# Packing the heads' sums and root broadcasts into quarters of TensorE, and swapping the rotation's halves by DMA, in a two-layer hybrid decoder

## The reference, cut to what matters

```python
def _head_rmsnorm(y, g, n_heads):
    yh = y.reshape(b, l, n_heads, w // n_heads)
    yh = yh * lax.rsqrt(jnp.mean(yh * yh, axis=-1, keepdims=True) + NORM_EPS)
    return yh.reshape(b, l, w) * g
# mLSTM, for each head:
    num = s @ v                                   # s: masked scores x weights
    den = sum(s, axis=-1)
    h_cell = num / maximum(abs(den), exp(-m_t))
# retention turns its queries and keys, halves (x1, x2) of each head:
    x1 * cos - x2 * sin,  x1 * sin + x2 * cos
# gated outputs, and the merge of the four branches:
    silu(r) * norm(gla);  sigmoid(o) * norm(h_cell);  silu(g) * norm(ret)
    merged = sum_n sigmoid(logits[n] + b) * (branch[n] @ w_branch[n])
```

## Time and profile before

| | |
|---|---|
| median of 3 runs | 1001.17 us (1001.13 to 1002.32) |
| the profiled execution, its own time | 1002.59 us |
| its span, first to last instruction | 1000.8 us |
| TensorE, matmuls | 984.6 us busy, 98% of the span |
| TensorE, weight loads | 933.9 us |
| VectorE | 592.3 us, 59% |
| ScalarE | 519.9 us, 52% |
| GpSimd | 85.0 us, 8% |
| DMA | 156.43 MB, 156 GB/s on the mean |
| granted clock of TensorE, mean | 0.996 |

### The profile page before, as it was taken

How to read it: one execution, slowest core, us unless ns; L and a number is a source line. 1 busy time by engine, 2 the same in 40 slices (tenths; PEclk the granted TensorE clock), 3 DMA queues, 4 the chain that set the end, 5 groups by cost and what they waited for, 6 DMA issues and landing times.

```text
span 1000.8 us, 19677 instructions
## 1 busy us (share of the span) xinstructions
PE 984.6 (98%) x7722; PEld 933.9 (93%) x7722; DVE 592.3 (59%) x903; ACT 519.9 (52%) x832; POOL 85.0 (8%) x78
## 2 busy tenths in 40 slices
PE   8999999999999999999999999999999999999997
PEld 6999888889998999999979998888999899999996
DVE  7556565356866655553465565744578566556443
ACT  5543754365466544444455437544754755555442
POOL 1000000000031221110100000000000322221010
PEclk9999999999999999999999999999999999999999
DMA  6864434346552655555545544344464546565551
GB/s 179 280 209 142 125 114 126 91 121 168 170 172 84 207 168 170 173 191 163 165 127 168 169 145 126 110 126 127 128 168 169 169 128 209 171 202 172 190 189 42
DMA packets 168525, 156.43 MB, mean 156 GB/s; under 512 B 9092, under 2 KB 167023, under 8 KB 168079
## 3 DMA queue, kind: packets, MB, share of 16 engines
q1 hardware_dynamic: 167598, 152.13, 49.2%
q10 hardware_dynamic: 672, 3.37, 1.0%
q0 software_dynamic: 192, 0.07, 0.0%
HBM read 154.50 MB, written 1.05 MB: 155 GB/s over the span
## 4 chain that ended last, share of the span: by engine, by line
PE 92%; DVE 3%; ACT 3%; DMA 1%; issue 1%; DVEq 0%; SPq 0%; ACTq 0%
PE banks L627 26%; PE banks L629 25%; PE banks L628 25%; PE banks L677 2%; PE banks L662 1%; PE banks L658 1%; PE banks L659 1%; PE banks L876 1%; ACT hi L1050 1%; DVE lo L1391 1%; PE banks L874 1%; PE banks L607 1%; PE banks L903 1%; DVE sub L1419 1%; PE banks L911 1%
## 5 line engine op out<-in xcount | busy, mean ns | idle before, releaser
L627 PE MATMUL banks<-xh,hi 128*128 128x272 f32 (+1 forms) x1584 | 461.0, 291 | 0.2
L629 PE MATMUL banks<-xh,lo 128*128 128x272 f32 (+1 forms) x1584 | 453.9, 287 | 0.0
L628 PE MATMUL banks<-xl,hi 128*128 128x272 f32 (+1 forms) x1584 | 452.4, 286 | 0.0
L1391 DVE TENSOR_TENSOR lo<-raw,hi 128x1024 fp32r<-128x1024 f32 (+1 forms) x290 | 349.4, 1208 | 173.3 <-ACT hi L1050 172.1
L1050 ACT ACTIVATE hi<-raw 128x1024 fp32r<-128x1024 f32 (+1 forms) x290 | 301.9, 1042 | 106.7 <-PE banks L629 58.6
L627 PEld LDWEIGHTS banks<-xh,hi 128*128 128x128 f32 x1584 | 298.9, 189 | 6.5 <-issue 4.1
L628 PEld LDWEIGHTS banks<-xl,hi 128*128 128x128 f32 x1584 | 298.9, 189 | 0.6
L629 PEld LDWEIGHTS banks<-xh,lo 128*128 128x128 f32 x1584 | 298.9, 189 | 0.0
L629 PE MATMUL banks<-ah,lo 128*128 128x272 f32 (+1 forms) x352 | 100.5, 285 | 0.0
L627 PE MATMUL banks<-ah,hi 128*128 128x272 f32 (+1 forms) x352 | 100.2, 285 | 0.0
L628 PE MATMUL banks<-al,hi 128*128 128x272 f32 (+1 forms) x352 | 100.1, 284 | 0.0
(11 more groups left out here) (261 smaller groups left out, 1150.9 us busy)
## 6 DMA issues: line engine op xcount, KB each, us to landing
raw<-in_w_in SPq DMA_DIRECT2D x54, 1024.0 KB, 5.3
raw<-in_ffn_w_gate SPq DMA_DIRECT2D x22, 1024.0 KB, 5.3
raw<-in_ffn_w_up SPq DMA_DIRECT2D x22, 1024.0 KB, 5.3
raw<-in_ffn_w_down SPq DMA_DIRECT2D x16, 1024.0 KB, 5.1
raw<-in_w_out SPq DMA_DIRECT2D x8, 1024.0 KB, 5.1
raw<-in_w_in SPq DMA_DIRECT2D x12, 512.0 KB, 4.3
raw<-in_w_branch SPq DMA_DIRECT2D x12, 512.0 KB, 5.4
raw<-in_ffn_w_down SPq DMA_DIRECT2D x8, 768.0 KB, 4.4
```

The source lines that it names most:

```text
L627: mm(dst, wh, mh, start=start, stop=False)
L628: mm(dst, wh, ml, start=False, stop=False)
L629: return mm(dst, wl, mh, start=False, stop=stop)
L1391: tt(lo[g % 2][:, 0:k, f], raw[g % 2][:, 0:k, f], hi[g % 2][:, 0:k, f].bitcast(F32), ALU.subtract).then_inc(lo_ready, 2 if g in G_MIX else 1)
```

## The change

Five things, in both layers:

1. Denominators: each head sums into its own 32 columns of the array and lands in row 32h of the bank, in three rounds of four matmuls. All four heads must be ready first. Row vectors sit at partitions 32h from here on, and the operations of ScalarE and VectorE on them run over 128 partitions. exp(-m) is brought to those partitions by four DMAs that ScalarE issues; the other rows are set to 1.
2. Mean squares: two rounds of four matmuls with 32 output columns, rows 32h for mLSTM and 32h + 1 and 32h + 2 for the others.
3. Root broadcasts: all six behind logit 19, two that read 64 rows and four that read 32, into six banks.
4. Rotation: eight DMAs a layer on SP's queue swap the halves into `sa` and `sb2`; no matmul.
5. In layer 1 the projections `gr`, `rg` and `mo`, and the outputs' norm and rounding, run from position 16 on.

```diff
+QUERY_ONLY = ("gr", "rg", "mo")
+SWAP_BEHIND = {"rv": "rq", "sbq": "rk"}
@@ BEHIND
-    19: [("headbc", 0)],
-    20: [("headbc", 1)],
...
-    24: [("headbc", 5)],
+    19: [("headbc",)],
@@ block.sync
+            def swap(l, name):
+                for j in range(2):
+                    wait_taken(sp, group_tile(l, name) + j)
+                for at in range(0, P, HD):
+                    for to, src in ((at, at + 32), (at + 32, at)):
+                        sp.dma_start(turned_of(name)[to:to + 32, :, 0:T], M[name][src:src + 32, :, :]).then_inc(swapped[name], 16)
...
                         load(g, cols(w_in[l], c))
+                    if name in SWAP_BEHIND:
+                        swap(l, SWAP_BEHIND[name])
@@ block.tensor
-                    features(t + j, g, j, xh, xl, 0)
+                    features(t + j, g, j, xh, xl, group_start(l, name))
...
-            def rot(l, i):
...
-                mm(rot_banks[i % 2][:, 0:T], cut["perm"], M[name][:, i % 2, :], start=True, stop=True).then_inc(rot_ready[l], 1)
...
             def ml_den(l):
-                den = c3("denind", 4)
-                wait_p(l, ML, 0)
-                mm(e0[0:4, 0:T], cut["denind0"], M["pt0"][:], start=True, stop=False)
                 for h in range(HEADS):
                     wait_p(l, ML, h)
-                    mm(e0[0:4, KB1:T], den[:, h, :], M["pt"][:, h, 0:256], start=False, stop=False)
-                    last = mm(e0[0:4, KB2:T], den[:, h, :], M["pt"][:, h, 256:SCW], start=False, stop=h == 3)
+                for h in range(HEADS):
+                    mm(e0[quad[h], 0:T], cut["denind"][quad[h], :], M["pt0"][quad[h], :], start=True, stop=False)
+                for h in range(HEADS):
+                    mm(e0[quad[h], KB1:T], cut["denind"], M["pt"][:, h, 0:256], start=False, stop=False)
+                for h in range(HEADS):
+                    last = mm(e0[quad[h], KB2:T], cut["denind"], M["pt"][:, h, 256:SCW], start=False, stop=True)
...
             def headsum(l):
-                for p in range(6):
-                    pe.wait_ge(osq_ready[l], 6)
-                    last = mm(ps[0:12, 0:T], c3("headsum", 6)[:, p, :], osq[:, p, :], start=p == 0, stop=p == 5)
+                total = c3("headsum", 3)
+                pe.wait_ge(osq_ready[l], 6)
+                for g in range(HEADS):
+                    mm(ps[quad[g], 0:T], total[:, g % 2, :], osq[:, g // 2, :], start=True, stop=False)
+                for g in range(HEADS):
+                    last = mm(ps[quad[g], 0:T], total[:, 2, :], osq[:, 2 + g, :], start=False, stop=True)
...
+                for p in range(6):
+                    rows = slice(HD * p, HD * p + HD) if p < 2 else quad[p - 2]
+                    mm(spread_banks[p][:, 0:T], c3("headbc", 6)[rows, p, :], M["rows"][rows, 0, :], start=True, stop=True).then_inc(spread_ready[l], 1)
@@ block.scalar, ml_em
+                for h in range(HEADS):
+                    act.dma_start(rows[32 * h:32 * h + 1, 1, :], rows[32 + h:33 + h, 0, :]).then_inc(em_spread, 16)
@@ block.vector, rot
-                dve.wait_ge(rot_ready[l], i + 1)
-                tt(turned, rot_banks[i % 2][:, 0:T], cut["sin"], ALU.mult).then_inc(rot_free[l], 1)
+                dve.wait_ge(swapped[name], 64 * (l + 1))
+                tt(turned, turned, cut["sin"], ALU.mult).then_inc(rot_sin[l], 1)
@@ ml_rows
+                nc.vector.memset(rows[:, 1, :], 1.0).then_inc(ml_dve[l], 1)
```

More of the change, by code:

```diff
@@ L80 @@
 DOWN_K = (8, 8, 6)
-CONSTS = [("ident", 128), ("mean", 128), ("eps", 1), ("negtri", 128), ("negones", 128), ("perm", 128), ("negtri0", 32),
+CONSTS = [("ident", 128), ("mean", 128), ("eps", 1), ("negtri", 128), ("negones", 128), ("negtri0", 32),
           ("mask_lt", SCW), ("neg_lt", SCW), ("neg_le", SCW), ("mask_le", SCW),
@@ L120, in constants @@
     c["sin"][:] = np.tile(np.concatenate([-np.sin(ang), np.sin(ang)]), (2, 1))
-    other = np.where(p % HD < half, p + half, p - half)
-    c["perm"][other, p] = 1
+    c["headsum"][:HD, 0] = c["headsum"][HD:, 32] = 1.0 / HD
+    c["headsum"][:HD, 64 + 1] = c["headsum"][HD:, 64 + 2] = 1.0 / HD
     for pair in range(6):
         for i in range(P):
-            j = 2 * pair + i // HD
-            c["headsum"][i, pair * 12 + j] = 1.0 / HD
-            c["headbc"][j, pair * P + i] = 1
+            c["headbc"][head_row(pair, i // HD), pair * P + i] = 1
+    c["denind"][:, 0] = 1
     for h in range(HEADS):
-        c["denind"][:, h * 4 + h] = 1
-        c["denind0"][:, h] = head == h
         c["negind"][32 + h, h] = -1
@@ L337, in build @@
         glaref = sb("glaref", [P, 4])
[L338 removed]
+        dm2 = sb("dm2", [P, T])
         ones = sb("ones", [P, T])
@@ L932, in _ @@
             parts = {
-                "first": first, "group": group, "turn": turn, "gate": gate, "rot": rot, "logit": logit, "headsum": headsum, "headbc": headbc,
+                "first": first, "group": group, "turn": turn, "gate": gate, "logit": logit, "headsum": headsum, "headbc": headbc,
                 "sb_scores0": sb_scores0, "sb_scores": sb_scores,
@@ L1231, in den_abs_ @@
                 act.wait_ge(den_ready, l + 1)
-                act.wait_ge(ml_em, l + 1)
-                fn(M["rows"][0:4, 0, :], e0[0:4, 0:T], ACT.Abs).then_inc(den_abs, 1)
+                act.wait_ge(em_spread, 64 * (l + 1))
+                fn(M["rows"][:, 0, :], e0[:, 0:T], ACT.Abs).then_inc(den_abs, 1)
             def head_square(l, p):
@@ L1240, in head_rstd @@
             def head_rstd(l):
-                r = M["rows"][0:12, 0, :]
+                r = M["rows"][:, 0, :]
                 wait_taken(act, TILE[l][("headsum",)])
@@ L1247, in round_y @@
             def round_y(l, n):
-                fn(yh[:, n, :], M["osb"][:, n, :], ACT.Copy).then_inc(yh_ready[l], 1)
+                q0 = q_start(l)
+                fn(yh[:, n, q0:], M["osb"][:, n, q0:], ACT.Copy).then_inc(yh_ready[l], 1)
             def y_plain(l):
@@ L1639, in head_var @@
                 dve.wait_ge(den_dve[l], 2)
-                taken(stt(M["rows"][0:12, 0, :], dm2[:], EPS, bank_of(t)[0:12, 0:T], ALU.mult, ALU.add), t)
+                taken(stt(M["rows"][:, 0, :], dm2[:], EPS, bank_of(t)[:, 0:T], ALU.mult, ALU.add), t)
             def rest_of_y(l, i, n):
                 dve.wait_ge(yh_ready[l], i + 1)
-                tt(yl[:, n, :], M["osb"][:, n, :], yh[:, n, :].bitcast(F32), ALU.subtract).then_inc(yl_ready[l], 1)
+                q0 = q_start(l)
+                tt(yl[:, n, q0:], M["osb"][:, n, q0:], yh[:, n, q0:].bitcast(F32), ALU.subtract).then_inc(yl_ready[l], 1)
             def y_plain(l):
@@ L1658, in y_rest @@
                     dve.wait_ge(mo_ready, l + 1)
-                tt(osb[:, n, :], osb[:, n, :], M[gate][:, n % 2, :], ALU.mult).then_inc(y_step[l], 1)
+                tt(osb[:, n, q0:], osb[:, n, q0:], M[gate][:, n % 2, q0:], ALU.mult).then_inc(y_step[l], 1)
                 rest_of_y(l, p + 2, n)
```

73 lines of the change are left out of this document (37 added, 36 removed).

## The result

The changed kernel takes 990.21 us (989.43 to 991.24, 4 runs), the one before 1001.75 beside it (4 runs): ratio 0.9883, 95% interval 0.987 to 0.9897. That is 11.5 us less, where 14.6 were forecast, and above the upper end of the range, 989.8. The way was right, the size was not. Part of the miss of the range is the starting point: the forecast went out from 1001.17 us, and the kernel before came out at 1001.75 once its fourth run was in. As a difference the range ended at 11.4 us, so 11.5 lies barely inside it, which is luck; the gain is still some 3 us short. The two profiled executions differ by 12.2 us, and what follows accounts for that pair.

What follows compares the result with a forecast made beforehand. TensorE was taken as the bound; savings of 3.68 + 3.36 + 3.34 + 2.90 + 1.32 = 14.60 us took the median of 1001.17 us to 986.6, range 984.6 to 989.8 (forecast's own 984.6 to 988.4, chance 0.80).

Steps and rivals of the forecast that it cites:

- What bounds the kernel: Whole kernel: TensorE, busy 984.6 of 1000.8 us; a microsecond off it in the mixer moves everything behind forward by one.
- Rotation: Mixer, both layers: eight `perm` matmuls leave TensorE, four pairs of 0.92 us, 3.68 us saved.
- Denominators: Denominator block: 3.15 us a layer becomes three rounds of 0.59, 0.56 and 0.32; 3.36 us saved in all.
- mean squares: Mean-square block: six matmuls, 2.85 us a layer, become two rounds of 0.59; 3.34 us saved in all.
- Broadcasts: Root broadcasts: six matmuls of 0.46 a layer become one block of 1.31 us; 2.90 us saved in all.
- Columns: Projections gr, rg, mo in layer 1: 256 instead of 272 columns, 0.22 us less for six tiles, 1.32 us.
- ScalarE gets four DMA issues: Behind `ml_em`: 1.5 us of issues, mostly covered by ScalarE's idle 1.21 us before its next eviction; cost 0.
- the swaps: Rotation's DMAs on SP: first swap down near 71, about 1 us before VectorE wants it; cost 0.
- VectorE's pace behind the broadcasts: Six logits behind the broadcasts: VectorE falls behind 0.25 us a step in layer 1; cost 0, the thinnest cover.
- (a): Rival, broadcasts or denominators' round one: row tiles don't overlap, 2.6 or 2.5 us lost, 989.2, both 991.7; chance 0.10.
- (b): Rival, broadcast steps: the helpers become the bound, TensorE takes VectorE's 3.05 us; 1.5 to 3 us, 988 to 990; chance 0.05.
- (c): Rival, rotation: swaps land late, TensorE runs dry; at 24 us each the kernel stands near 1002 to 1004; chance 0.03.

Runs made afterwards that it cites:

- the version on SP: The changed kernel with the four DMAs of exp(-m) issued by SP instead of ScalarE: 988.79 us, ratio 0.9871 to the kernel before.

## Why the prediction was wrong

**What bounds the kernel** was right: TensorE's time went straight to the end, stretch by stretch.

**The terms on TensorE** came to 14.1 us against 14.60. Rotation 3.68, as read. Denominators 3.53 for 3.36, mean squares 3.64 for 3.34: a round with one of the same shape behind it costs 0.46 to 0.48, not 0.56 or 0.59; the rest of the 0.59 is the gap at a change of shape. Broadcasts 2.16 for 2.90: 0.4 of it are gaps at changes of shape (0.6 a block, not 0.3), the rest that a broadcast standing apart cost 0.41 in layer 1, not 0.46. Columns 1.10 for 1.32: 0.18 us a tile. The bounds held where they were given.

**The step that failed** is "ScalarE gets four DMA issues (0.37 apiece as on SP, 1.5 us) ... 0". The four took 3.25 and 3.58 us, 0.8 to 0.9 apiece on the mean: I had priced them by SP's issue of a weight load, a row of another kind. I had also looked for cover only up to the next eviction and its bank, and in layer 0 alone; the values' bank behind it had 2.7 us in layer 1, enough for 1.5 us and too little for 3.58. It cost 1.2 us in the profiled run; the version on SP gains 1.4 in the median.

**What no step held**: 0.8 us in the down projections, from tiles that moved by a few hundred bytes as the constants shrank. The forecast took every stretch that the change doesn't name as unchanged.

**The pair of traces adds up**: 14.1 from the terms, less 1.19 behind `ml_em`, 0.80 in the down projections and 0.24 in the output projection of layer 1, with 0.30 for the input, is 12.2 us.

**Costed at nothing and right**: the swaps as far as VectorE and the loads go (no wait; whether they lengthen ScalarE's issues is open), the wait for all four heads (no wait of TensorE), operations over 128 partitions (0.44 us instead of 0.43), VectorE's pace behind the broadcasts (its idle time for them gone, branch 0 not late). The output projection of layer 1 gave 0.24 back. ScalarE waits for weight loads there, but no run was made to show that as the cause.

**The rivals.** (a) fell on both sides: the row tiles overlap. The Trainium skill's rule (page TensorEngine Tiling (Array Packing), section Gotcha 1: PSUM Pressure) does not hold for these four tiles as far as time goes: 0.59 us in one bank. (b) did not happen. (c) did not happen, and its price was summed wrongly: by its own cover, swaps of 24 us each would be 7.4 us late, 29.6 for the four, which gives 1016 us and not 1002 to 1004. With both causes taken away the kernel stands at 987.95, 14.0 below its neighbour: the sum of the terms, within its noise. The range left no room for a cost on ScalarE or in a stretch that the change doesn't touch.

## What to carry to other kernels

Tiles side by side in the array cost one matmul a round here, 0.46 us for 272 columns, and 0.1 to 0.2 us more at each change of shape, so put rounds of one shape together. Price a DMA issue by a row of the same kind on the same queue. Keep it off an engine that empties TensorE's banks: SP's queue, which only issues DMAs, carried it for nothing here. Look for the cover at every bank behind the delay and in every layer. When a table in SBUF changes its length, compare stretches that the change doesn't touch; padding it back is the test.

## What the runs showed of the hardware that I had not expected

- Matmuls reading tiles moved by 128 bytes in SBUF started every 0.1267 instead of every 0.1255 us on the mean: 52.6 us instead of 51.9 for the same work, the same to 0.01 us in every trace.
- Four DMA issues of one row each took ScalarE 2.45 to 3.58 us and SP 2.5, against 0.37 us for one load of a megabyte on SP.
- With waits of TensorE of 2.4 and 2.9 us its clock stood at half for 3 and 6 us, which cost as much as the waits. Behind waits of 0.8 us for the same bank it did not fall.
